# Differential attention with softmax weights left unnormed, value products by tokens and a sub-norm per partition; rotary embedding on a bank copied to SBUF

## The chip, the cores and the metric

The kernel runs on one core of a Trainium2 chip. The metric is device time in microseconds (us) for one execution, the median of several. An execution has five engines that run at the same time, each through its own list of instructions in order: TensorE (PE in the profile, with PEld for its weight loads), VectorE (DVE), ScalarE (ACT), GpSimd (POOL) and SyncE (SP, which issues the DMAs). They wait for each other by semaphores only.

## What is computed

Two transformer stacks on 512 tokens of width 1024, in 32-bit floats: a feed-forward block, a mixing block (differential attention with 8 heads, dilated window attention with 12 heads, gates), a second feed-forward block, then two more layers (window attention with pooling, an MLP, latent attention with a recurrence, an MLP). The change touches the mixing block, whose first part is

```python
qa = partial_rope(qa)            # 8 heads x 2 parts x 64, only the first 16 of 64 rotate
ka = partial_rope(ka)
s = einsum('bqhcd,bkhcd->bhcqk', q, k) / 8        # two score matrices per head
p = softmax(s, axis=-1)
a = p[:, :, 0] - lam * p[:, :, 1]
oa = einsum('bhqk,bkhe->bqhe', a, v)              # v is 128 wide per head
oa = rmsnorm(oa, g_subln) * 0.8                   # over the 128 of each head and token
```

## The kernel before

Activations are kept transposed (features on partitions, 512 tokens along the free axis). Products with weights are made in three matmuls with high and low parts: the weights come from DRAM in chunks, ACT copies a chunk to its high part (`split`, L1733, 128x1024), DVE subtracts for the low part (L1953), and PE runs `mm` (L1532, L1534, L1536). Four split chunks are kept; the split of chunk c+3 is listed when the product of chunk c begins and needs chunk c-1 to be used up.

**Who sets the order.** `work_order()` writes one list of steps. Every engine goes through the same list and picks its part of each step, so the order of the list is the order in each engine's queue. In attention the list is woven from two sources. `pipeline()` advances units of attention; `fill(n)` advances a generator that makes projections (`stream_diff` here) so that PE has other work between the parts of a unit.

**Differential attention** is 32 units (8 heads times 4 blocks of 128 queries), from `diff_unit`. One unit has these steps:

- `diff_score`: PE makes the two 128x512 score matrices in two banks (L1613, each f32 matmul is two passes). DVE takes the maximum of each row (L2104, twice) and scales it (L2106). ACT exponentiates both banks with the row sums accumulated (L1793, twice).
- `diff_soft`: DVE takes the reciprocals of the two sums (L2111), multiplies one with lambda (L2114), scales the first matrix (L2115, 128x512) and adds the second times its factor (L2117, 128x512).
- `turn`: PE transposes the four 128x128 blocks (L1648) into bank 6; ACT copies them to a buffer `et` in `tmps` (L1817).
- `diff_out`: PE multiplies (L1655, four matmuls of two passes) with the value block as stationary and `et` as moving operand, so that the result has the 128 value features on partitions. The four blocks of a head fill one bank.
- After a head, `subln`: ACT copies the bank (L1823) and squares it (L1744), PE sums over partitions with a column of ones (L1589, 8 instructions), DVE makes the inverse root from small 128x4 operands (`rstd`, L1973 to L1984, 12 instructions in a chain), PE spreads it over partitions (L1598, 8 instructions), DVE multiplies (L2179), ACT makes the high part (L1827), DVE the low part (L2182).

`pipeline(..., 1, 1, av=4)` lists, per turn n: score of unit n, one filler step, soft of unit n-1, out of unit n-4, pieces of a finished head's sub-norm, transposes of unit n-2, one filler step. Each turn so takes 2 filler steps.

**The filler** is 22 projections of 128 features (`qk_tile`): for each 24 matmuls into one of two banks, then `rope`. One projection is three steps: 12 matmuls, 12 matmuls, and the rotation. In `rope` DVE multiplies the bank with the cosine table (L2092) and shuffles the bank's partitions (`stream_shuffle`, L2093); then the bank is free. POOL multiplies by the sine table (L2379) and adds (L2385). The two buffers `ftmps` are single: the next rotation starts when the last has ended. Nine filler steps (three projections) are run before unit 0. The same `qk_tile` feeds the dilated attention that follows (`stream_dil`, six projections among four gates), whose own units are not touched.

## Time and profile before

| what | value |
| --- | --- |
| median of 3 runs | 2631.23 us (2629.97 to 2632.77) |
| the profiled execution | 2631.93 us, its span 2630.1 us |
| mean granted TensorE clock | 0.966 |
| PE busy | 2469.7 us, 94% |
| DVE busy | 1321.2 us, 50% |
| ACT busy | 931.6 us, 35% |
| POOL busy | 243.7 us, 9% |
| differential attention, first score to the next stage's first matmul | 461.24 to 701.66 us |

The span runs from the first to the last instruction, and about 1.8 us of the execution lie around it. A row of the trace names an engine, a line of the kernel, the tile written and those read. "Idle before" is time in which the engine stood still ahead of such instructions, with the instruction whose end released it. PE instructions overlap, so the distance from one start to the next is their cost; an f32 matmul shows as two instructions. L numbers are lines of the kernel before.

### The profile page before, as it was taken

To read this page: it belongs to the slowest core of one execution; us is meant where nothing else is said; L and a number is where in the kernel's file an instruction comes from. 1 tells how busy PE (TensorE), PEld (TensorE's weight loads), DVE (VectorE), ACT (ScalarE), POOL (GpSimd) and SP (SyncE) were. 2 spreads that over 40 slices of the span, in tenths; PEclk is the share of its full clock that TensorE was granted. 3 is DMA by queue.
4 is the path that set the end of the run, shared out by engine and by line. 5 is a ranking of instruction groups with operands and counts; after the bars stand their busy time and mean duration, and the time that the engine had idled before them with its cause. 6 is when DMAs were issued, how large, how long until landed. Compare 5 with 4: busy or idle time off the path is not lost.

```text
span 2630.1 us, 28659 instructions
## 1 busy us (share of the span) xinstructions
PE 2469.7 (94%) x11256; PEld 1968.9 (75%) x11256; DVE 1321.2 (50%) x2175; ACT 931.6 (35%) x1446; POOL 243.7 (9%) x180
## 2 busy tenths in 40 slices
PE   8999989989899998999998789999998788999998
PEld 6888877666677787888887557888886556888886
DVE  5423345777554444532436665524445777542433
ACT  4333223343333323322223344413322655431331
POOL 0100102221001001100102200000000211000000
PEclk9999999999899998999998889999998898999999
DMA  4233223111111132223322112322221011332221
GB/s 142 93 100 105 84 86 100 58 44 41 43 62 52 55 102 80 88 86 115 96 83 89 49 40 84 106 96 96 96 88 34 30 32 51 104 104 96 90 99 69
DMA packets 66902, 208.38 MB, mean 79 GB/s; under 512 B 7440, under 2 KB 16144, under 8 KB 66512
## 3 DMA queue, kind: packets, MB, share of 16 engines
q1 hardware_dynamic: 66768, 206.55, 24.5%
q8 instruction: 90, 1.47, 0.2%
q14 instruction: 44, 0.36, 0.0%
HBM read 204.42 MB, written 2.10 MB: 79 GB/s over the span
## 4 chain that ended last, share of the span: by engine, by line
PE 77%; DVE 11%; issue 7%; ACT 3%; POOL 1%; DMA 0%; SPq 0%; DVEq 0%; POOLq 0%; ACTq 0%
PE bank L1532 23%; PE bank L1536 23%; PE bank L1534 22%; DVE wlo L1953 1%; PE bank L1648 1%; DVE sm L2104 1%; ACT whi L1733 1%; PE bank L1569 1%; PE bank L1598 1%; PE bank L1571 1%; PE bank L1573 1%; PE bank L1589 1%; PE bank L1613 1%; DVE eb L2115 1%; PE bank L1639 1%
## 5 line engine op out<-in xcount | busy, mean ns | idle before, releaser
L1953 DVE TENSOR_TENSOR wlo<-wraw,whi 128x1024 fp32r<-128x1024 f32 (+4 forms) x438 | 481.4, 1101 | 570.1 <-ACT whi L1733 568.2
L1532 PE MATMUL bank<-hhi,whi 128*128 128x512 f32 x1744 | 703.1, 403 | 25.9 <-DVE ftmps L2093 13.8
L1534 PE MATMUL bank<-hlo,whi 128*128 128x512 f32 x1744 | 688.7, 395 | 2.5 <-DVE hlo L1959 2.5
L1536 PE MATMUL bank<-hhi,wlo 128*128 128x512 f32 x1744 | 689.1, 395 | 0.7 <-DVE wlo L1953 0.5
L1733 ACT ACTIVATE whi<-wraw 128x1024 fp32r<-128x1024 f32 (+4 forms) x438 | 409.6, 936 | 492.6 <-PE bank L1536 448.0
L1532 PEld LDWEIGHTS bank<-hhi,whi 128*128 128x128 f32 x1744 | 332.9, 191 | 118.5 <-issue 44.5
L1536 PEld LDWEIGHTS bank<-hhi,wlo 128*128 128x128 f32 x1744 | 332.8, 191 | 75.4 <-DVE wlo L1953 3.0
L1534 PEld LDWEIGHTS bank<-hlo,whi 128*128 128x128 f32 x1744 | 333.6, 191 | 74.2 <-DVE hlo L1959 4.5
L1532 PE MATMUL bank<-mhi,whi 128*128 128x512 f32 x576 | 227.1, 394 | 0.1
L1536 PE MATMUL bank<-mhi,wlo 128*128 128x512 f32 x576 | 225.8, 392 | 0.0
L1534 PE MATMUL bank<-mlo,whi 128*128 128x512 f32 x576 | 223.6, 388 | 0.2 <-DVE mlo L2204 0.2
L1536 PEld LDWEIGHTS bank<-mhi,wlo 128*128 128x128 f32 x576 | 108.1, 188 | 25.3
L1534 PEld LDWEIGHTS bank<-mlo,whi 128*128 128x128 f32 x576 | 108.1, 188 | 24.7 <-DVE mlo L2204 0.5
L1532 PEld LDWEIGHTS bank<-mhi,whi 128*128 128x128 f32 x576 | 108.3, 188 | 22.0 <-ACT mhi L1840 0.5
L2358 POOL TENSOR_TENSOR tmps<-tmps 128x512 f32<-128x512 f32 x44 | 56.6, 1286 | 551.0 <-DVE tmps L2005 482.5
L1765 ACT ACTIVATE tmps<-tmps 128x512 f32<-128x512 f32 x64 | 40.5, 632 | 184.1 <-DVE tmps L2023 184.1
L2379 POOL TENSOR_TENSOR ftmps<-ftmps,rs 128x512 f32<-128x512 f32 (+1 forms) x39 | 57.8, 1481 | 508.8 <-DVE ftmps L2093 508.8
L2018 DVE TENSOR_TENSOR ya<-ya,bank 128x512 f32<-128x512 f32 x64 | 43.8, 685 | 115.0 <-PE bank L1536 115.0
L1648 PE MATMUL bank<-ident,eb 128*128 128x128 f32 x400 | 67.3, 291 | 35.6 <-ACT tmps L1817 17.8
L2026 DVE TENSOR_TENSOR mlo<-tmps,mhi 128x512 fp32r<-128x512 f32 x64 | 44.3, 693 | 87.2 <-ACT mhi L1768 87.2
L1793 ACT ACTIVATE eb<-bank,sm 128x512 f32<-128x512 f32 x64 | 43.5, 684 | 118.0 <-DVE sm L2106 118.0
L1648 PEld LDWEIGHTS bank<-ident,eb 128*128 128x128 f32 x400 | 46.3, 147 | 49.8 <-issue 26.8
(344 smaller groups left out, 3266.4 us busy)
## 6 DMA issues: line engine op xcount, KB each, us to landing
wraw<-in_stream SPq DMA_DIRECT2D x343, 512.0 KB, 3.5
wraw<-in_stream SPq DMA_DIRECT2D x40, 192.0 KB, 2.3
wraw<-in_stream SPq DMA_DIRECT2D x22, 256.0 KB, 2.6
wraw<-in_stream SPq DMA_DIRECT2D x8, 320.0 KB, 2.9
xa<-in_x SPq DMA_DIRECT2D x8, 256.0 KB, 5.7
out<-ya SPq DMA_DIRECT2D x8, 256.0 KB, 2.6
m<-in_mask SPq DMA_DIRECT2D x1, 1024.0 KB, 5.1
wraw<-in_stream SPq DMA_DIRECT2D x8, 128.0 KB, 2.0
```

The lines of the kernel that those rows point to most:

```text
L1532: pe.matmul(out, sh, xh, start=first, stop=False)
L1534: pe.matmul(out, sh, xl, start=False, stop=False)
L1536: p = pe.matmul(out, sl, xh, start=False, stop=end and last)
L1648: p = pe.transpose(banks[tb][:, i * 128:i * 128 + 128], src[:, at0:at0 + 128], ident[:, :])
L1733: act.activation(whi[j][:, 0:L], wraw[i][:, 0:L], F.Copy).then_inc(*hi.up(c))
L1765: act.activation(tmps[:, q, :], tmps[:, q, :], F.Square).then_inc(*relu_sq.up((s, f)))
L1793: act.activation(buf(("eb", es[c])), banks[bs[c]][:, :], F.Exp, bias=SM(r, 2 + c), scale=SC, accum_out=SM(r, 4 + c)).then_inc(*exp.up(("di ...
L1953: dve.tensor_tensor(wlo[j][:, 0:L], wraw[i][:, 0:L], whi[j][:, 0:L].bitcast(f32), SUB).then_inc(*lo.up(c))
L2018: dve.tensor_tensor(ya[:, n, :], ya[:, n, :], banks[b][:, :], ADD).then_inc(*x_dve.up((nxt, n)))
L2026: dve.tensor_tensor(ahl[s][1][:, f % 16, :], tmps[:, q, :], ahl[s][0][:, f % 16, :].bitcast(f32), SUB).then_inc(*v_lo.up((s, f)))
L2358: pool.tensor_tensor(tmps[:, q, :], tmps[:, q, :], tmps[:, u, :], MUL).then_inc(*gated.up((s, f)))
L2379: pool.tensor_tensor(s, s, rs[rows, :], MUL).then_inc(*rope_sin.up(key))
```

## The change

1. **Softmax weights unnormed.** ACT's first row sum is kept for the head in a new small tensor `hc`. DVE no longer scales the first matrix (L2115 goes); it multiplies lambda, the first sum and the reciprocal of the second, and adds the second matrix times that to the first. The result is the wanted one times the first row sum; the root mean square norm takes that factor out again, with its small constant scaled by the square of the sum.
2. **One maximum for both banks.** The eight banks are one tensor, and one `tensor_reduce` with two results takes the place of two.
3. **Value products by tokens.** `diff_out` has the `et` block as stationary and the value block as moving operand, so that the result has queries on partitions.
4. **Sub-norm per partition.** After each `diff_out` ACT copies the 128x128 result to `tmps` and squares it into a scratch with the sum accumulated. Per head DVE makes the inverse root from 128x4 operands (`sub_root`: two instructions and the same 11 that `rstd` has after its first), ACT scales the four blocks (`sub_scale`), PE transposes them into bank 6, ACT makes the high part and DVE the low part from that bank with the gain (`sub_turn`). The sums and the spreading on PE, L1823, L1744 and L2179 go.
5. **Rotation on a copied bank.** ACT copies the projection's bank to `ftmps`, which frees the bank; DVE shuffles from there; POOL does sine product, cosine product and sum, three instructions.
6. **A new order.** `pipeline` isn't used for these units. `diff_exp` is a step of its own. Per turn n the list is: score of n, 1.2 filler steps, exponentials of n, transposes of n-1, 1.2 filler steps, out of n-1, soft of n, then the next piece of a finished head's sub-norm (`sub_root` in the turn with the head's last out, `sub_scale` and `sub_turn` in the turn after). A projection is four steps of 6 matmuls, the last with the rotation. Nine filler steps before unit 0 are now two projections and a quarter.

The diff, cut to its core (the marks, the new small tensors, and `root`, which holds the unchanged instructions of `rstd`, are left out; HC(h, name, i, n) are columns of `hc`):

```diff
@@ -585,12 +585,27 @@
         t.freed(("shuffled", key))
         return (name, key)
 
+    def rope_copied(kind, key, t, after):
+
+        r, s = FT.take(), FT.take()
+        put("rope_copied", kind, key, t.bank, r.i, s.i, (t.end, *r.was, *s.was), after)
+        r.free = s.free = (("roped", key),)
+        t.freed(("rope_in", key))
+        return ("roped", key)
+
     def qk_tile(key):
         while QK.full():
             yield
         q = QK.take()
-        t = yield from feat([key], ("h", 1))
-        q.tok = rope(("qk", q.i), key, t, q.was)
+        t = Tile(G.take(), ("h", 1), 128, 0)
+        c = opened(key)
+        for kk in range(0, 8, 2):
+            put("mm", t, c, kk, kk + 2, kk, True)
+            if kk < 6:
+                yield
+        closed.add(c)
+        t.end = ("used", c)
+        q.tok = rope_copied(("qk", q.i), key, t, q.was)
         done[key] = q
         yield
 
...
@@ -612,10 +627,11 @@
         qs, ks = ensure(("qa", h, 0)), ensure(("ka", h, 0))
         es, r = [EB.take(), EB.take()], SMR.take()
         bs = [SB.take(), SB.take()]
-        put("diff_score", u, qs.i, ks.i, [b.i for b in bs], r.i, [e.i for e in es],
-            (qs.tok, ks.tok), [b.was for b in bs], r.was, [e.was for e in es])
+        put("diff_score", u, qs.i, ks.i, [b.i for b in bs], r.i, (qs.tok, ks.tok), [b.was for b in bs], r.was)
         if i == 3:
             qs.free = ks.free = (("score", ("diff", u, 1)),)
+        yield
+        put("diff_exp", u, [b.i for b in bs], r.i, [e.i for e in es], [e.was for e in es])
         for c in range(2):
             bs[c].free = (("exp", ("diff", u, c)),)
         yield
@@ -624,38 +640,45 @@
         yield
         et = T.take()
         yield from turn("diff", u, es[0], 4, et, (("soft", ("diff", u)),))
-        yield
         if i == 0:
-            heads[h] = MB.take()
-        out = heads[h]
-        put("diff_out", u, et.i, out.i, out.was)
+            heads[h] = MB.take(), T.take()
+        out, o = heads[h]
+        put("diff_out", u, et.i, out.i, out.was, o.i, o.was)
         et.free = (("out", ("diff", u)),)
         if i == 3:
-            late.append(subln(h, out))
-
...
+            late.append(subln(h, o))
+
+    def subln(h, o):
+        put("sub_root", h)
+        yield
+        put("sub_scale", h, o.i)
+        tb = TB.take()
+        put("sub_turn", h, o.i, tb.i, tb.was)
+        tb.free = (("oa_lo", h),)
+        o.free = (("sub_turn", h),)
+        yield
+
+    def after_heads():
+        for l in list(late):
+            if next(l, 0) == 0:
+                late.remove(l)
+
+    last, owed = None, 0.0
+    for unit in [diff_unit(h, i) for h in range(8) for i in range(4)] + [None]:
+        for l, fills in ((unit, 1.2), (unit, 0), (last, 1.2), (last, 0), (unit, 0)):
+            if l:
+                next(l, None)
+            owed += fills
+            fill(int(owed))
+            owed -= int(owed)
+        after_heads()
+        last = unit
     fill(10 ** 6)
+    for l in late:
+        for _ in l:
+            pass
+    late.clear()
     va_free = (("out", ("diff", (7, 3))),)
 
     share_banks(6)
...
@@ -1648,13 +1681,21 @@
                         p = pe.transpose(banks[tb][:, i * 128:i * 128 + 128], src[:, at0:at0 + 128], ident[:, :])
                     p.then_inc(*turn.up((stage, u, c)))
                 elif k == "diff_out":
-                    (h, i), et, ob, was = a
+                    (h, i), et, ob, was, o, owas = a
                     w.wait_ge(*turned["diff", (h, i), 0])
                     waits((("tm_act", ("va", 1, 3)), ("tm_dve", ("va", 1, 2)), *was))
                     for kt in range(4):
-                        p = pe.matmul(banks[ob][:, i * 128:i * 128 + 128], va_v[:, kt, h * 128:h * 128 + 128],
-                                      tmps[:, et, kt * 128:kt * 128 + 128], start=kt == 0, stop=kt == 3)
+                        p = pe.matmul(banks[ob][:, i * 128:i * 128 + 128], tmps[:, et, kt * 128:kt * 128 + 128],
+                                      va_v[:, kt, h * 128:h * 128 + 128], start=kt == 0, stop=kt == 3)
                     p.then_inc(*out_mm.up(("diff", (h, i))))
...
+                elif k == "sub_turn":
+                    h, o, tb, was = a
+                    waits(was)
+                    for i in range(4):
+                        w.wait_ge(*sub_scaled[h, i])
+                        p = pe.transpose(banks[tb][:, i * 128:i * 128 + 128], tmps[:, o, i * 128:i * 128 + 128],
+                                         ident[:, :])
+                    p.then_inc(*sub_turn.up(h))
...
                 elif k == "diff_score":
-                    u, q, kq, bs, r, es, toks, bwas, rwas, ewas = a
+                    pass
+                elif k == "diff_exp":
+                    (h, i), bs, r, es, ewas = a
+                    w.wait_ge(*maxed["diff", (h, i)])
+                    if h > 1:
+                        w.wait_ge(*sub_root[h - 2])
                     for c in range(2):
-                        w.wait_ge(*maxed["diff", u])
                         waits(ewas[c])
                         act.activation(buf(("eb", es[c])), banks[bs[c]][:, :], F.Exp, bias=SM(r, 2 + c), scale=SC,
-                                       accum_out=SM(r, 4 + c)).then_inc(*exp.up(("diff", u, c)))
+                                       accum_out=SM(r, 5) if c else HC(h, "sum", i, 1)).then_inc(
+                                           *exp.up(("diff", (h, i), c)))
+                elif k == "diff_out":
+                    (h, i), et, b, was, o, owas = a
+                    at0 = i * 128
+                    w.wait_ge(*out_mm["diff", (h, i)])
+                    waits(owas)
+                    act.activation(tmps[:, o, at0:at0 + 128], banks[b][:, at0:at0 + 128],
+                                   F.Copy).then_inc(*sub_in.up((h, i)))
+                    act.activation(junk[:, :], banks[b][:, at0:at0 + 128], F.Square,
+                                   accum_out=HC(h, "sq", i, 1)).then_inc(*sub_sq.up((h, i)))
+                elif k == "sub_scale":
+                    h, o = a
+                    w.wait_ge(*sub_root[h])
+                    for i in range(4):
+                        s = tmps[:, o, i * 128:i * 128 + 128]
+                        w.wait_ge(*sub_in[h, i])
+                        act.activation(s, s, F.Copy, scale=HC(h, "root", i, 1)).then_inc(*sub_scaled.up((h, i)))
+                elif k == "sub_turn":
+                    h, o, tb, was = a
+                    w.wait_ge(*sub_turn[h])
+                    w.wait_ge(*dcols_set[0])
+                    act.activation(oahi[:, h, :], banks[tb][:, :], F.Copy, scale=DC(16)).then_inc(*oa_hi.up(h))
...
+                elif k == "sub_root":
+                    h, = a
+                    v, u, r = HC(h, "var"), HC(h, "u"), HC(h, "root")
+                    w.wait_ge(*sub_sq[h, 3])
+                    if h > 1:
+                        w.wait_ge(*sub_scaled[h - 2, 3])
+                    dve.scalar_tensor_tensor(u, HC(h, "sum"), EPS, HC(h, "sum"), MUL, MUL).then_inc(*chain.up())
                     w.wait_ge(*chain.now())
-                    dve.tensor_scalar(r.bitcast(i32), r.bitcast(i32), -1.0, 1597463007.0, MUL, ADD).then_inc(*chain.up())
...
-                        dve.scalar_tensor_tensor(u, u, -0.5, v, MUL, MUL).then_inc(*chain.up())
-                        w.wait_ge(*chain.now())
-                        dve.scalar_tensor_tensor(r, u, 1.5, r, ADD, MUL).then_inc(*(rstd.up(norm) if it == 2
-                                                                                    else chain.up()))
+                    dve.scalar_tensor_tensor(v, HC(h, "sq"), 1.0 / 128, u, MUL, ADD).then_inc(*chain.up())
+                    w.wait_ge(*chain.now())
...
+                elif k == "rope_copied":
+                    kind, key, b, ri, si, was, after = a
+                    w.wait_ge(*rope_in[key])
+                    waits(was)
+                    dve.stream_shuffle(ftmps[:, si, :], ftmps[:, ri, :], rope_of(kind)[2]).then_inc(*shuffled.up(key))
                 elif k == "diff_score":
-                    u, q, kq2, bs, r, es, toks, bwas, rwas, ewas = a
+                    u, q, kq2, bs, r, toks, bwas, rwas = a
                     waits(rwas)
-                    for c in range(2):
-                        w.wait_ge(*score["diff", u, c])
-                        dve.tensor_reduce(SM(r, c), banks[bs[c]][:, :], AX.X, MAX).then_inc(*chain.up())
+                    w.wait_ge(*score["diff", u, 1])
+                    assert bs[1] == bs[0] + 1
+                    dve.tensor_reduce(SM(r, 0, 2), bank[:, bs[0]:bs[0] + 2, :], AX.X, MAX).then_inc(*chain.up())
                     w.wait_ge(*chain.now())
                     dve.tensor_scalar(SM(r, 2, 2), SM(r, 0, 2), -SC, None, MUL).then_inc(*maxed.up(("diff", u)))
                 elif k == "diff_soft":
                     u, r, es = a
                     e0, e1 = buf(("eb", es[0])), buf(("eb", es[1]))
                     w.wait_ge(*exp["diff", u, 1])
-                    dve.reciprocal(SM(r, 6, 2), SM(r, 4, 2)).then_inc(*chain.up())
+                    dve.reciprocal(SM(r, 6), SM(r, 5)).then_inc(*chain.up())
                     w.wait_ge(*chain.now())
                     w.wait_ge(*lam[0])
-                    dve.tensor_scalar(SM(r, 7), SM(r, 7), DC(17), None, MUL).then_inc(*chain.up())
-                    dve.tensor_scalar(e0, e0, SM(r, 6), None, MUL).then_inc(*chain.up())
+                    dve.scalar_tensor_tensor(SM(r, 7), HC(u[0], "sum", u[1], 1), DC(17), SM(r, 6), MUL,
+                                             MUL).then_inc(*chain.up())
                     w.wait_ge(*chain.now())
                     dve.scalar_tensor_tensor(e0, e1, SM(r, 7), e0, MUL, ADD).then_inc(*soft.up(("diff", u)))
...
+                elif k == "sub_turn":
+                    h, o, tb, was = a
                     w.wait_ge(*oa_hi[h])
-                    dve.tensor_tensor(oalo[:, h, :], tmps[:, o, :], oahi[:, h, :].bitcast(f32), SUB).then_inc(*oa_lo.up(h))
+                    dve.scalar_tensor_tensor(oalo[:, h, :], banks[tb][:, :], DC(16), oahi[:, h, :].bitcast(f32), MUL,
+                                             SUB).then_inc(*oa_lo.up(h))
...
+                elif k == "rope_copied":
+                    kind, key, b, ri, si, was, after = a
+                    dst, rows, _, tab = rope_of(kind)
+                    r, s = ftmps[:, ri, :], ftmps[:, si, :]
+                    w.wait_ge(*shuffled[key])
+                    w.wait_ge(*at(tab))
+                    w.wait_ge(*before.now())
+                    pool.tensor_tensor(s, s, rs[:, :], MUL).then_inc(*rope_sin.up(key))
+                    before = rope_sin
+                    w.wait_ge(*before.now())
+                    pool.tensor_tensor(r, r, rc[:, :], MUL).then_inc(*rope_r.up(key))
+                    before = rope_r
+                    w.wait_ge(*rope_r[key])
+                    waits(after)
+                    pool.tensor_tensor(dst, r, s, ADD).then_inc(*roped.up(key))
+                    before = roped
```

## Rows read from the trace of the kernel before

**Rows 1.** The page's busy time by engine.

```profile
PE 2469.7 (94%) x11256; PEld 1968.9 (75%) x11256; DVE 1321.2 (50%) x2175; ACT 931.6 (35%) x1446; POOL 243.7 (9%) x180
```

**Rows 2.** Stretches: busy us of each engine, PE clock, DMA share, GB/s.

```profile
461.00:680.00 219.00, 199.79 (x1022) 145.59 (x1020) 173.21 (x376) 88.08 (x190) 52.08 (x40) 0.98 0.15 47
680.00:702.00 22.00, 14.81 (x77) 14.08 (x78) 10.01 (x38) 5.99 (x12) 0.00 (x0) 0.71 0.00 1
```

**Rows 3.** Waits, 455 to 695 us: total us, times, longest us.

```profile
DVE wlo L1953 <- ACT whi L1733: 25.4, 11, 2.5
...
PE bank L1532 <- DVE ftmps L2093: 13.8, 8, 2.6
```

**Rows 4.** Groups of instructions, 455 to 695 us: busy us, mean ns, idle before.

```profile
L2115 DVE TENSOR_SCALAR eb<-eb,sm 128x512 f32<-128x512 f32 x32 | 26.7, 836 | 0.0
L1953 DVE TENSOR_TENSOR wlo<-wraw,whi 128x1024 fp32r<-128x1024 f32 x20 | 24.4, 1220 | 25.4 <-ACT whi L1733 25.4
...
L2093 DVE STREAM_SHUFFLE ftmps<-bank 128x512 f32<-128x512 f32 x21 | 15.3, 728 | 0.0
...
L1598 PE MATMUL bank<-ident,sm 128*128 128x128 f32 x56 | 8.5, 300 | 2.0 <-DVE ftmps L2093 2.0
...
L1589 PE MATMUL bank<-ones,ssb 128*128 128x1 f32 x56 | 7.4, 253 | 0.0
```

**Rows 5.** PE in order of time: half a projection, out, transposes, the next.

```profile
564.51 0.50 PE L1532 MATMUL bank<-hhi,whi 128*128 128x512 f32 x1
...
567.41 1.05 PE L1655 MATMUL bank<-tmps,ya 128*128 128x128 f32 x8
568.30 0.60 PE L1648 MATMUL bank<-ident,eb 128*128 128x128 f32 x4
568.65 0.48 PE L1532 MATMUL bank<-hhi,whi 128*128 128x512 f32 x1
```

**Rows 6.** All engines in order of time, 571 to 582 us, one score onward.

```profile
571.60 1.13 PE L1613 MATMUL bank<-qk 64*128 64x512 f32 x4
...
572.83 1.29 DVE L2104 TENSOR_REDUCE sm<-bank 128x1 f32<-128x512 f32 x2 [1.02 <-PE bank L1613]
...
574.36 0.69 ACT L1793 ACTIVATE eb<-bank,sm 128x512 f32<-128x512 f32 x1 [3.61 <-DVE sm L2106]
...
575.65 1.29 POOL L2379 TENSOR_TENSOR ftmps<-ftmps,rs 128x512 f32<-128x512 f32 x1 [7.70 <-DVE ftmps L2093]
575.70 0.60 ACT L1817 ACTIVATE tmps<-bank 128x512 f32<-128x512 f32 x1
575.78 1.44 DVE L2115 TENSOR_SCALAR eb<-eb,sm 128x512 f32<-128x512 f32 x1
576.18 1.06 ACT L1733 ACTIVATE whi<-wraw 128x1024 fp32r<-128x1024 f32 x1
577.02 1.35 POOL L2385 TENSOR_TENSOR qk<-ftmps 128x512 f32<-128x512 f32 x1
577.26 1.66 DVE L2117 SCALAR_TENSOR_TENSOR eb<-eb,sm 128x512 f32<-128x512 f32 x1
578.84 0.15 DVE L1973 TENSOR_SCALAR sm<-bank 128x4 f32<-128x4 f32 x1
...
581.01 0.16 DVE L1984 SCALAR_TENSOR_TENSOR sm<-newt,sm 128x4 f32<-128x4 f32 x1
```

**Rows 7.** L2117 over the whole run: ns min/median/max, first and last start.

```profile
L2117 DVE SCALAR_TENSOR_TENSOR eb<-eb,sm x32: 750/752/1669, 473.5 to 684.1; 128x512 f32<-128x512 f32 x32
```

**Rows 8.** POOL's product when it meets L1953, at 452 us.

```profile
451.84 2.16 POOL L2379 TENSOR_TENSOR ftmps<-ftmps,rs 128x512 f32<-128x512 f32 x1 [44.30 <-DVE ftmps L2093]
```

**Rows 9.** The only ACT copies of 128x128 out of a bank.

```profile
L1866 ACT ACTIVATE ve<-bank,rcs x4: 360/368/377, 1458.5 to 1459.3; 128x128 f32<-128x128 f32 x4
```

**Rows 10.** PE at the end of the stage.

```profile
699.93 2.08 PE L1598 MATMUL bank<-ident,sm 128*128 128x128 f32 x8 [2.44 <-DVE sm L1984]
```

**Rows 11.** A wait of the dilated stage, 775 to 905 us.

```profile
PE bank L1624 <- POOL qk L2385: 2.9, 1, 2.9
```

More of the change, by code:

```diff
@@ L1243, in program @@
         newt = sb("newt", [128, 8])
[L1244 removed]
+        bank = ctx.enter_context(nc.psum_tensor("bank", [128, 8, 512], f32))
+        banks = [bank[:, i, :] for i in range(8)]
         ahl = {}
```

75 lines of the change are left out of this document (31 added, 44 removed).

## The prediction, made before the change was run

> **What bounds the kernel now.** I first read the page's busy times: PE is busy 94% of the run, so elsewhere the kernel is a matmul kernel and only work that PE does, or waits for, counts [rows 1]. Then the stretches of the stage that is changed. From the first score at 461 us to 680 us PE is busy 199.8 of 219 us and DVE 173.2 [rows 2]. From 680 to 702 the filler has run out: PE is busy 14.8 of 22 us at a granted clock of 0.71, POOL has nothing, and the stage ends with the last spreading [rows 2, 10]. Third, who waits: PE waited 13.8 us for the shuffle that frees a projection's bank, and DVE waited 25.4 us for ACT's split, which stands behind the exponentials in ACT's queue [rows 3]. So PE is short of the bound of its own work because DVE's queue runs late, and the last 22 us have no cover.
>
> PE's own work in the stage, by starts: 12 projection matmuls take 567.41-564.51 = 2.90 us, so a new filler step (6) takes 1.45; out 0.89; transposes 0.35; two scores about 1.1 [rows 5, 6]. 32 units at 2.34 are 75 us; 79 new filler steps 114.5.
>
> **What is removed.** DVE: L2115, 26.7 us in all; the cosine products, 21 of about the shuffle's 0.73, 15 us; a 512-wide multiply per head, about 0.7 each, 5 [rows 4]. One maximum over two banks takes what two took (1.29), so it saves next to nothing [rows 6]. PE: sums and spreading, 7.4 + 8.5 us for seven heads, against 0.4 per head for the new transposes: 13 us less [rows 4, 5]. Turning the operands of the value product costs nothing: eight 128x128 passes either way. The filler: 79 steps remain after the first nine, and 33 turns at 2.4 take 79.2, so the 22 us tail gets cover. If PE were the bound, all this would be worth 40 us or more.
>
> **What is added or moved.** (1) POOL does three instructions of 1.3 us per projection where it did two, some 4.1 us in a row [rows 6]. (2) ACT gets a 0.6 us bank copy per projection, two 128x128 instructions per unit and four per head. The nearest row has 0.37 each, and (1459.3-1458.5)/3 = 0.27 from start to start [rows 9]. (3) The order is much shallower: transposes and out of unit n-1 stand behind the exponentials of n on ACT, and the maximum of n+1 stands behind soft of n on DVE. Before, soft used exponentials of a turn ago and out was four turns behind.
>
> **A turn, walked along the queues.** Score start to exponentials is 574.36-571.60 = 2.76; two exponentials 1.34; the copy of the transposes 0.60; out 0.89. The next score follows: 5.6 us for a quiet turn, against PE's own 5.8 on average, so no slack is left [rows 5, 6]. Into this loop fall 20 projection ends and 19 splits. A projection's end puts a 0.6 bank copy on ACT and a 0.73 shuffle on DVE ahead of soft; a split puts 1.06 on ACT, then 1.22 on DVE (wlo), ahead of soft too where it comes in the second filler place, as two of three do [rows 4, 6]. Soft is 2.6 from the exponentials' start to where DVE is free (1.5 for both sums, 0.45 small ones, 0.67 of L2117), and the next maximum has to wait for it.
>
> **POOL holds DVE up.** L2115 began at 575.78, while POOL ran 575.65 to 576.94, and took 1.44; L2117 began at 577.26 inside POOL's next one and took 1.66, where its minimum is 0.75 [rows 6, 7]. Both ended about 0.3 and 0.55 us after POOL's. The reverse holds: POOL's product took 2.16 when DVE's wlo was in front [rows 8]. So wlo and L2117 each lose about 0.9 us when they meet a rotation, and rotations now last 4.1 of about 11 us. The Trainium skill ("GPSIMD Engine Reference", Key points) says that GpSimd shares its SBUF interfaces with VectorE and contends with instructions with two SBUF inputs; by that rule the small 128x4 and 128x1 ones with two inputs would be held as well, which no row here shows. Counting them would add up to 1.3 us at some turns and make the sum some 10 us larger; I leave them free.
>
> With that the five turns of the repeating pattern (12 filler steps, three projections) come to: quiet 5.6; end of a projection before the exponentials and a split after them 8.2; an end in the second place 7.8; a split in the first place 6.0; end and split in the second place 8.7. The last as an example, from the score's start: transposed copy done 4.7, bank copy 5.2, shuffle 5.95, split 6.1, POOL's first product to 7.3, wlo to 8.3, POOL's second to 9.5, L2117 to 10.1, where a quiet turn's next maximum begins at 6.8. Sum 36.3 for five, 7.25 each; without any holding 33, 6.6 each. 32 turns: 232 us (211).
>
> **Heads.** `sub_root` waits on DVE for the last square: out + 0.95, two ACT instructions and an accumulator read, 0.8. Then 13 small instructions at the pace of rstd (12 in 581.17-578.84 = 2.3) take 2.5 [rows 6], with the next maximum queued behind: 2.2 us late. `sub_turn` stands on PE straight behind the next out and waits for two 128x128 and four scalings on ACT: out + 0.95 + 0.8 + 1.2, then 0.4, where the next score would be at 0.89: 2.4 us of idle PE, less what DVE was late anyway, plus 0.3 for the low part on DVE: 1.6. 3.8 per head, seven heads: 27 us. On the pieces, the nearest small row gives 0.27 to 0.37 each; at 0.69 each (a full-width one) [rows 6] heads would cost 10 us more, at nothing 10 less.
>
> The Trainium skill ("VectorE: DVE Perf Modes", the section on the TRN2 errata) gives ScalarE reading a bank 172 cycles plus one per element and advises pieces of 512 or more; at its 1.2 GHz that estimates 0.25 us for 128 wide, close to the 0.27 pace [rows 9]. It speaks against cutting one 512-wide copy, square and scaling into twelve pieces; with its figure heads would cost 1 us less.
>
> **Start and end.** The nine steps end 4 us sooner, near 457, but score 0 waits for the second rotation: projection end near 455.7, copy 0.6, shuffle 0.73, POOL 4.1, and 0.9 lost to wlo in each of two rotations: score 0 near 463. PE stands about 6 us. The last turn and its chain (two filler places, out, squares, root, scaling, transposes) take 9 us where 22 went.
>
> **Sum.** 463 + 232 + 27 + 9 = 731 against 702: +29. In the dilated stage a score waited 2.9 us for a rotation [rows 11]; that rotation is now 1.3 + 0.6 - 0.7 longer and the four of the burst before it keep 5.8 us apart instead of 5.5: +2 to +3. Some head delays fall in turns already late: -4. So +28 on the profiled execution's 2631.9, 2660; the median shown is 0.7 lower: 2659. DMAs are the same in number and order, SP's queue is untouched.
>
> **Rivals.**
> *Faster: cover wins.* If holding is small and ACT's and DVE's extras fit beside PE's work, the turn is PE's 5.8: 463 + 186 + 2.4 x 7 + 9 = 675, -27: 2604. With the clock that was 0.71 in the tail back up this is its full size. For it: DVE sheds some 45 us, and its lateness is what held PE. Against: the loop over ACT is 5.6 alone. It decides at the second filler place: if wlo and shuffle come ahead of an idle DVE, not ahead of a late soft. Half of it (turn 6.4) is still -5. Chance 0.27.
> *Nothing: no holding.* Turn 6.6: 463 + 211 + 25 + 9 = 708, with overlap about 0 to +8. Chance 0.13, half of it within 0.2%.
> *Worse: the small ones are held as well.* `sub_root`'s 13 and the lambda product wait for POOL, turns near 7.7 and heads near 5: +50 and more, 2685. Chance 0.07.
> *Forecast:* waits across ACT, DVE and POOL take PE's place, +10 to +50. Chance 0.53.
>
> **How the numbers follow.** A measurement tells 0.2% (5.3 us) from no change. Faster: 0.27. Within: 0.06, half the second rival. Slower: 0.67, the rest. The range leaves out about a fifth: its low end is 2608, nearly all of the faster case's mechanism but its last 4 us, its high end 2686, the third rival's value. The likeliest case alone is 2641 to 2682.
>
> **What would show it.** In the profile after: the stage from first score to first value matmul 265 to 275 us long; PE busy near 75% in it with idle ahead of the out product (L1655's successor) ended by ACT's transposed copy, some 1 us per unit, and ahead of the sub-norm's transposes, some 2 us each for eight; DVE busy below 150 us and idle behind exponentials; L2117's successor with a mean above 1.1 us; wlo with a maximum near 2.1; the first score after 462. It is wrong if PE waits on these under 30 us in total, if turns average 6 us, or if the granted clock of the stage drops and does more than the waits.

## The result and the profile after

| what | before | after |
| --- | --- | --- |
| median | 2630.6 us (2628.3 to 2632.8) | 2683.7 us (2683.4 to 2684.3) |
| the profiled execution, its span | 2631.93, 2630.1 us | 2683.37, 2681.6 us |
| mean granted TensorE clock | 0.966 | 0.959 |
| PE, DVE, ACT, POOL busy | 2469.7, 1321.2, 931.6, 243.7 us | 2482.9, 1314.3, 963.7, 287.4 us |
| first score to the next stage's first matmul | 461.24 to 701.66 us | 462.69 to 750.72 us |

The change makes the kernel slower: after over before is 1.0203, with an interval of 1.0191 to 1.0215, or +53 us. The stage itself grew from 240.4 to 288.0 us, +47.6. Another 1.5 us lie ahead of it. In the dilated stage a score waits 7.2 us for a rotation (L1657 for L2481), where it waited 2.9 [rows 11].

The stretches of after, the stage first and then the work ahead of it (busy time and instructions of each engine, then the granted clock, DMA share, GB/s):

```profile
463.00:751.00 288.00, 229.28 (x1019) 154.22 (x1018) 177.24 (x330) 122.35 (x334) 86.52 (x60) 0.90 0.11 35
440.00:463.00 23.00, 15.39 (x68) 12.18 (x68) 9.67 (x11) 6.58 (x8) 9.37 (x6) 0.95 0.28 91
```

The same view of before, from 461 to 702 us:

```profile
461.00:702.00 241.00, 214.60 (x1099) 159.66 (x1098) 183.22 (x413) 94.07 (x202) 52.08 (x40) 0.95 0.14 42
```

PE stands idle for 288.0 - 229.3 = 59 us, where it was 26: +32. The other +15 is PE's busy time, though PE has less to do. This is the clock: 0.90 where it was 0.95. By these two figures, PE was at the slower of its two levels (1.2 GHz, half of 2.4) for about 58 us of the stage, and for about 24 before; that is an estimate. At the slower level the four score instructions that took 1.13 us at 605.33 take 2.08 at 618.95, in the rows in order of time below. Everything else in this comparison is a question of who makes PE wait.

The waits of after from 455 to 770 us (the engine that stood, then whose instruction ended it: us in total, times, the longest):

```profile
ACT eb L1842 <- DVE sm L2190: 99.2, 26, 7.1
DVE ftmps L2182 <- ACT ftmps L1832: 47.6, 20, 5.8
PEld bank L1688 <- ACT tmps L1888: 45.0, 27, 5.2
PE bank L1688 <- ACT tmps L1888: 33.7, 21, 4.8
...
PE bank L1696 <- ACT tmps L1860: 13.0, 8, 6.6
PE bank L1681 <- DVE eb L2201: 11.8, 11, 2.1
...
PE bank L1646 <- POOL qk L2481: 6.0, 1, 6.0
```

PE's waits are new ones beside [rows 3]. The largest is the out product (L1688) for ACT's copy of the transposed weights (L1888), then the sub-norm's transposes (L1696) for ACT's scaling, then the transposes (L1681) for DVE's sum of the two matrices (L2201), and once the first score for a rotation. PEld, the weight load of the same product, stands at the same places. PE no longer waits for the shuffle; in its place DVE waits 47.6 us for the copy that now precedes the shuffle.

The groups of the same stretch (busy us, mean ns of one | idle before):

```profile
L2188 DVE TENSOR_REDUCE sm<-bank 128x2 f32<-128x1024 f32 x32 | 39.0, 1220 | 22.7 <-PE bank L1646 22.7
...
L2201 DVE SCALAR_TENSOR_TENSOR eb<-eb,sm 128x512 f32<-128x512 f32 x32 | 37.3, 1165 | 1.1
...
L2031 DVE TENSOR_TENSOR wlo<-wraw,whi 128x1024 fp32r<-128x1024 f32 x23 | 32.6, 1415 | 24.3 <-ACT whi L1774 24.3
...
L2198 DVE SCALAR_TENSOR_TENSOR sm<-hc,dcols,sm 128x1 f32<-128x1 f32 x32 | 25.7, 804 | 1.1
...
L1850 ACT ACTIVATE tmps<-bank 128x128 f32<-128x128 f32 x32 | 8.9, 277 | 29.4 <-PE bank L1688 29.4
L1852 ACT ACTIVATE junk<-bank 128x128 f32<-128x128 f32 x32 | 8.7, 272 | 0.0
...
L2060 DVE SCALAR_TENSOR_TENSOR hc<-hc 128x4 f32<-128x4 f32 x8 | 5.6, 701 | 3.3 <-ACT junk L1852 3.2
```

The fourth row is the one to stop at: the product with lambda, one element per partition, takes 804 ns in the mean. ACT's small pieces cost what was said, 0.28 and 0.27. The product in its own view (min/median/max in ns):

```profile
L2198 DVE SCALAR_TENSOR_TENSOR sm<-hc,dcols,sm x32: 219/1054/1305, 467.9 to 736.9; 128x1 f32<-128x1 f32 x32
```

And one turn of after in order of time (start, us, engine, idle before in brackets), with a projection's end, a split, and then a finished head:

```profile
602.26 0.68 ACT L1842 ACTIVATE eb<-bank,sm 128x512 f32<-128x512 f32 x1
...
603.59 0.60 ACT L1888 ACTIVATE tmps<-bank 128x512 f32<-128x512 f32 x1
604.06 1.07 ACT L1774 ACTIVATE whi<-wraw 128x1024 fp32r<-128x1024 f32 x1
...
604.24 1.16 PE L1688 MATMUL bank<-ya,tmps 128*128 128x128 f32 x8 [0.68 <-ACT tmps L1888]
604.57 1.27 POOL L2477 TENSOR_TENSOR ftmps<-ftmps,rc 128x512 f32<-128x512 f32 x1
605.17 1.75 DVE L2031 TENSOR_TENSOR wlo<-wraw,whi 128x1024 fp32r<-128x1024 f32 x1 [2.02 <-ACT whi L1774]
...
605.33 1.13 PE L1646 MATMUL bank<-qk 64*128 64x512 f32 x4
...
605.92 2.15 POOL L2481 TENSOR_TENSOR qk<-ftmps 128x512 f32<-128x512 f32 x1
...
607.03 1.06 DVE L2198 SCALAR_TENSOR_TENSOR sm<-hc,dcols,sm 128x1 f32<-128x1 f32 x1
...
608.13 0.75 DVE L2201 SCALAR_TENSOR_TENSOR eb<-eb,sm 128x512 f32<-128x512 f32 x1
608.80 0.15 DVE L2060 SCALAR_TENSOR_TENSOR hc<-hc 128x4 f32<-128x4 f32 x1
...
611.25 1.22 DVE L2188 TENSOR_REDUCE sm<-bank 128x2 f32<-128x1024 f32 x1
...
612.71 0.69 ACT L1842 ACTIVATE eb<-bank,sm 128x512 f32<-128x512 f32 x1 [6.73 <-DVE sm L2190]
...
614.69 2.07 PE L1688 MATMUL bank<-ya,tmps 128*128 128x128 f32 x8 [2.35 <-ACT tmps L1888]
...
618.95 2.08 PE L1646 MATMUL bank<-qk 64*128 64x512 f32 x4
```

The exponentials were done at 603.6, but DVE began nothing on them until the split's low part was over (606.9). The lambda product then stood from 607.03 to 608.09, where POOL's instruction ended at 608.07. The score of 605.33 was ready near 606.5, and its maximum began at 611.25, behind the sum of the two matrices and the 13 small instructions of a head's root (608.80 to 611.3). ACT stood 6.73 us, and PE waited for the copy behind these exponentials.

### The profile page after: what moved, and what is told of

The parts are those of the page before. It is cut to its first block, busy times and chain, and to the rows that moved or that the text cites. A ratio compares the mean times of both kernels' runs of the same rounds, so it can differ in the third digit from the quotient of the medians.

```text
span 2681.6 us, 28469 instructions
## 1 busy us (share of the span) xinstructions
PE 2482.9 (93%) x11160; PEld 1961.6 (73%) x11160; DVE 1314.3 (49%) x2083; ACT 963.7 (36%) x1586; POOL 287.4 (11%) x208
## 4 chain that ended last, share of the span: by engine, by line
PE 76%; DVE 11%; issue 6%; ACT 5%; POOL 2%; DMA 1%; SPq 0%; DVEq 0%; ACTq 0%; POOLq 0%
PE bank L1565 22%; PE bank L1569 22%; PE bank L1567 22%; DVE wlo L2031 1%; PE bank L1681 1%; ACT whi L1774 1%; ACT eb L1842 1%; PE bank L1646 1%; PE bank L1688 1%; PE bank L1602 1%; PE bank L1604 1%; PE bank L1606 1%; DVE sm L2188 1%; PE bank L1709 1%; DVE sm L2198 1%
## 5 line engine op out<-in xcount | busy, mean ns | idle before, releaser
L2031 DVE TENSOR_TENSOR wlo<-wraw,whi 128x1024 fp32r<-128x1024 f32 (+4 forms) x438 | 489.3, 1119 | 562.0 <-ACT whi L1774 560.1
L1681 PE MATMUL bank<-ident,eb 128*128 128x128 f32 x400 | 68.0, 292 | 40.7 <-ACT tmps L1888 17.4
L1681 PEld LDWEIGHTS bank<-ident,eb 128*128 128x128 f32 x400 | 46.4, 146 | 62.6 <-issue 26.6
L2102 DVE SCALAR_TENSOR_TENSOR tmps<-bank,rb 128x512 f32<-128x512 f32 x64 | 44.1, 690 | 64.3 <-PE bank L1569 62.8
```

What stands on the lines that cost most here:

```text
L1681: p = pe.transpose(banks[tb][:, i * 128:i * 128 + 128], src[:, at0:at0 + 128], ident[:, :])
L2031: dve.tensor_tensor(wlo[j][:, 0:L], wraw[i][:, 0:L], whi[j][:, 0:L].bitcast(f32), SUB).then_inc(*lo.up(c))
L2102: dve.scalar_tensor_tensor(tmps[:, q, :], banks[b][:, :], 0.0, rb[:, :], MAX, MUL).then_inc(*relu.up((s, f)))
```

## The experiments

All of them count their stage from the first score to the first matmul of the next stage (240.4 us before, 288.0 after), and "over before" is the ratio to the kernel before on the same chip. Lengths of stages, busy and idle times are those of one profiled execution of each kernel.

**1. The lambda product with one tensor input.** On after:

```diff
-dve.scalar_tensor_tensor(SM(r, 7), HC(u[0], "sum", u[1], 1), DC(17), SM(r, 6), MUL, MUL)
+dve.tensor_scalar(SM(r, 7), HC(u[0], "sum", u[1], 1), DC(17), SM(r, 6), MUL, MUL)
```

> The changed kernel, with the 128x1 product of lambda (L2198, mean 0.80 us, minimum 0.22) as a tensor_scalar with two pointer scalars, so that it has one tensor input. Theory 1 (POOL holds DVE instructions with two tensor inputs, small ones too): its mean falls to about 0.22, but L2201 behind it now meets the same POOL instruction itself, so its mean rises from 1.17 towards 1.5 and the run gains 3 to 8 us. Theory 2 (the small product is slow for another reason, its wait on the reciprocal or a busy queue): its duration stays near 0.8. Theory 3 (being held is free time): duration falls, run unchanged within 2 us.

Measured 2669.6 us, 1.0160 over before (1.0143 to 1.0176), 0.43% or some 11 us less than after. The row now reads:

```profile
L2198 DVE TENSOR_SCALAR sm<-hc,dcols,sm x32: 271/273/277, 466.9 to 725.3; 128x1 f32<-128x1 f32 x32
```

With the same inputs as scalars it is never held. Its own time falls by 32 x 0.53 = 17 us, DVE's busy time in the stage only by 11 (177.2 to 166.4), since `wlo` is held more instead: its mean is 1536 ns where it was 1415. The sum behind the product (L2201) is held more often and for less each time (median 1279 where it was 752, mean 1158 where it was 1165). The stage falls by 11 us too, to 277.2.

**2. The old rotation, in the new order.** On after:

```diff
-        q.tok = rope_copied(("qk", q.i), key, t, q.was)
+        q.tok = rope(("qk", q.i), key, t, q.was)
```

> The changed kernel, with the rotation of before: DVE's cosine product and shuffle from the bank, two POOL instructions instead of three, no copy on ACT. Quarter steps and everything else stay. Theory 1 (POOL's three in a row hold DVE, and ACT's copy delays the exponentials): the first score comes 1.5 to 3 us sooner, turns shorten by 0.4 us, run 12 to 20 us faster than the change, 2664 to 2672. Theory 2 (the shallow order alone makes the loss; DVE's extra 0.69 us per projection costs as much as is saved): within 5 us of 2684.

Measured 2665.1, 1.0135 (1.0120 to 1.0150): 18 us less than after. The first score comes at 459.34, 3.4 us sooner, and the stage is 277.1 us, 10.9 shorter. The lambda product's mean falls from 804 to 645.

**3. The out product one turn later.** On after:

```diff
-    for unit in [diff_unit(h, i) for h in range(8) for i in range(4)] + [None]:
-        for l, fills in ((unit, 1.2), (unit, 0), (last, 1.2), (last, 0), (unit, 0)):
+    for unit in [diff_unit(h, i) for h in range(8) for i in range(4)] + [None, None]:
+        for l, fills in ((unit, 1.2), (unit, 0), (prev, 0), (last, 1.2), (unit, 0)):
...
-        last = unit
+        last, prev = unit, last
```

> The changed kernel with the value product of unit n-2 listed before the transposes of n-1, so that it no longer waits for the copy that ACT makes behind the exponentials of n. One turn is added at the end. Theory 1 (the loop score, maximum, exponentials, transposed copy, out, next score paces quiet turns at 5.6 us and PE's 79 us of waits for the copy are the loss): the waits of the value product for ACT's copy fall below 10 us, turns shorten by 0.7 to 1 us, run 20 to 30 us faster, 2655 to 2663. Theory 2 (DVE's queue paces: maximum behind soft behind split and shuffle): the wait moves to the transposes, which wait for soft, and the run gains under 8 us.

Measured 2666.3, 1.0144 (1.0127 to 1.0161): 15 us less. PE's wait of 33.7 us for L1888 is gone from the out product, and a part of it is found again at the sub-norm's transposes, 39.0 where it was 13.0:

```profile
PE bank L1696 <- ACT tmps L1860: 39.0, 8, 6.6
...
PE bank L1681 <- DVE eb L2201: 13.3, 10, 2.2
```

So a part of the stall went to the next thing that PE asks of ACT too soon, which is `sub_turn`. Of the 17.2 us that the stage is shorter (270.8), 6.4 are idle time of PE (52.3 us are left); the other 10.8 are its busy time, at a clock of 0.92 where it was 0.90.

**4. Part 1 alone, on before.** L2115 goes and lambda takes the first sum in the instruction that was there:

```diff
-dve.tensor_scalar(SM(r, 7), SM(r, 7), DC(17), None, MUL)
-dve.tensor_scalar(e0, e0, SM(r, 6), None, MUL)
+dve.tensor_scalar(SM(r, 7), SM(r, 7), DC(17), SM(r, 4), MUL, MUL)
```

> The kernel before with part 1 alone: DVE no longer scales the first softmax matrix (L2115, 26.7 us), the factor of the second is multiplied by the first sum in the same small instruction. The sub-norm's small constant is not scaled with the sum, as a part of the computation left out. Theory 1 (DVE's queue was what PE waited for before): 8 to 15 us faster than before, 2616 to 2623. Theory 2 (DVE waited for ACT's split anyway, so time saved there is spent waiting): within 4 us.

Measured 2621.2, 0.9974 (0.9960 to 0.9987): 27 us less of DVE's time give 7 us. DVE's wait for the split (L1953 for L1733, 455 to 770 us) rises from 47.1 to 55.5: a part of what is removed turns into waiting.

**5. The sub-norm's transposes one turn later.** On after:

```diff
         put("sub_scale", h, o.i)
+        yield
         tb = TB.take()
```

> The changed kernel with the head's transposes, high and low part listed one whole turn after ACT's scaling, nothing else. Theory 1 (PE stands about 2 us per head straight behind the scalings): PE's waits of L1696 for L1860 (13 us with the weight loads' 15) fall to the last head's 6, run 8 to 14 us faster than the change, near 2670. Theory 2 (the heads fall in turns that DVE has made late anyway, so the wait only moves to the transposes or the out product): under 4 us.

Measured 2666.7, 1.0135 (1.0119 to 1.0150): 18 us less. The stage:

```profile
461.49:735.36 273.87, 217.50 (x1019) 148.82 (x1019) 176.60 (x330) 121.53 (x334) 86.67 (x60) 0.94 0.12 38
```

PE's waits of L1696 fall from 13.0 to 6.6 us, all of it the last head's, but PE still waits 35.9 us for the transposed copy, and its idle time in the stage only falls from 58.7 to 56.4. What falls is its busy time for the same matmuls, from 229.3 to 217.5 us, at a clock of 0.94 where it was 0.90. So by these two executions nearly all of this gain is the clock's, and not the 1.6 us per head of the sum.

**6. Part 5 alone, on before.** The copied-bank rotation (ACT copy, DVE shuffle, three POOL instructions) takes the place of the old one; the order stays.

> The kernel before with part 5 alone: ACT copies the projection's bank, DVE shuffles from there, POOL makes three instructions. The old order, with out four turns behind, stays. Theory 1 (POOL's third instruction holds DVE's two-input ones whatever the order): L2115 and L2117 get means near 1.0 and 1.2, DVE saves 14.5 us of cosine products and loses as much or more, run 3 to 12 us slower than before. Theory 2 (the rotation harms only in the shallow order, and here the bank is freed sooner): 3 to 10 us faster than before, PE's 13.8 us of waits for the shuffle gone.

Measured 2654.1, 1.0084 (1.0066 to 1.0102): +23 us, more than in either theory. The waits that came with it:

```profile
DVE ftmps L2116 <- ACT ftmps L1800: 34.5, 19, 3.2
...
PE bank L1541 <- ACT ftmps L1800: 18.0, 8, 3.0
```

PE waited 13.8 us for the shuffle that freed a projection's bank [rows 3]. Now it waits 18.0 for the copy, and DVE, whose queue holds the shuffle, waits 34.5 for it as well, with the next maximum behind. A copy that is meant to free the bank sooner stands in ACT's queue behind two exponentials: of the stage's 19 copies every one starts straight behind these or behind the copy of the transposes.

**7. Part 1 with the filler spread.** Experiment 4 and `pipeline(..., 0.8, 0.8, av=4)` in place of 1, 1, so that the filler lasts to the end of the stage.

> The kernel before with part 1 alone and 0.8 filler steps where 1 was, at both places, so that the 57 steps last over all 36 turns. The sub-norm's small constant is left unscaled. Theory 1 (a slow last stretch without filler is worth its cover): the 20 us without filler work shrink to under 10, the clock stays up, and the run is 8 to 15 us faster than with part 1 alone, 15 to 20 us faster than before. Theory 2 (turns are paced by DVE, so fewer filler steps per turn leave PE idle in each turn and nothing is won): within 4 us of part 1 alone, 5 to 8 us faster than before.

Measured 2618.7, 0.9952 (0.9937 to 0.9967): -13 us, 6 more than in experiment 4, by ratios whose intervals overlap. From 680 to 700 us PE is now busy 15.8 of 20 us at a clock of 0.88; in experiment 4 it was 15.6 at 0.78. The stage takes 233.6 us here and 232.2 there. So the filler does reach the tail and the clock there is higher, but that this cover shortens anything is not shown: the stage as a whole, with less filler in each turn ahead of the tail, is no shorter.

**8. The four mends together.** After with the edits of 1, 2, 3 and 5.

> The changed kernel with four of its costs undone at once: lambda product with one tensor input, rotation as before, value product one turn later, the head's transposes one turn after the scalings. Theory 1 (the costs are separate): the gains of the single runs add, 11 + 16 + 15 + about 10, and it comes to 2628 to 2634, level with the kernel before. Theory 2 (they overlap, since each only shifts which queue is late): 2640 to 2652, still 0.5 to 0.9% slower than before. Theory 3 (with the waits gone PE's lighter work and the covered tail show): below 2615.

Measured 2617.5, 0.9946 (0.9931 to 0.9962): faster than before by 14 us. The single gains are 0.43 + 0.68 + 0.59 + 0.68 = 2.38%; together they are 1.0203 - 0.9946 = 2.57%. They add up within the intervals, so they are four losses rather than one seen four times. The stage is 226.7 us:

```profile
459.10:685.80 226.70, 203.55 (x1018) 144.68 (x1019) 165.83 (x350) 108.20 (x314) 55.25 (x40) 0.98 0.15 45
```

As many matmul rows as in after take 203.6 us instead of 229.3, and PE stands 23 us instead of 59: of the 61 us between the two stages, idle time is 36 and the clock 26.

**9. As 6, with the cosine product on DVE.** DVE multiplies the copy with the cosine table (0.69 us), and POOL has two instructions as before.

> The kernel before with the copied bank, but the cosine product on DVE, from the copy, so that POOL has two instructions as before. It splits the 22.6 us that the copied bank cost in the old order. Theory 1 (POOL's third instruction is the cost): it comes back to within 5 us of the kernel before. Theory 2 (the copy on ACT is: it queues behind the exponentials, so shuffle and bank come late, PE's 18 us of waits for it): the loss stays, 15 to 25 us slower than before, with DVE's extra 0.69 us per projection on top.

Measured 2656.7, 1.0102 (1.0087 to 1.0117): the loss of experiment 6 stays whole. Against the kernel before, DVE has the same work and POOL the same two instructions; what is new is the copy on ACT, and that DVE reads the copy instead of the bank. These two together cost 26 us. The second has a price as well: POOL's sine product, beside the cosine product that now has both inputs in SBUF, takes 1.79 us in the mean where it took 1.32. Against experiment 6, POOL's third instruction is exchanged for the cosine product on DVE, and nothing is won by it. The waits for the copy are the same:

```profile
DVE ftmps L2116 <- ACT ftmps L1800: 31.6, 19, 3.1
...
PE bank L1541 <- ACT ftmps L1800: 19.0, 8, 3.0
```

**10. Soft ahead of the second filler place.** On the kernel of experiment 8:

```diff
-        for l, fills in ((unit, 1.2), (unit, 0), (prev, 0), (last, 1.2), (unit, 0)):
+        for l, fills in ((unit, 1.2), (unit, 0), (prev, 0), (last, 0), (unit, 1.2)):
```

> The kernel of the four mends with soft of unit n listed ahead of the second filler place, so that DVE does it before the split's low part and the rotation listed there. Theory 1 (soft behind late filler work still delays the next maximum): 4 to 10 us faster than the four mends. Theory 2 (with the out product one turn later PE no longer feels it; the filler's own low parts now come later behind exponentials that DVE must wait for): within 3 us, or up to 5 slower.

Measured 2604.6, 0.9900 (0.9886 to 0.9914): 26 us faster than before, the fastest version here. The split's low part and the projection's instructions now come behind soft in DVE's queue, not ahead of it. The stage:

```profile
459.60:676.30 216.70, 201.69 (x1019) 143.36 (x1019) 169.95 (x350) 108.67 (x314) 59.32 (x40) 0.98 0.16 47
```

PE's own work is what it was in experiment 8; its idle time falls from 23 to 15 us. The mean of the sum of the two matrices falls from 1021 to 867 ns, so it is held less often (experiment 8's row, then this one's):

```profile
L2202 DVE SCALAR_TENSOR_TENSOR eb<-eb,sm 128x512 f32<-128x512 f32 x32 | 32.7, 1021 | 1.1
```

```profile
L2202 DVE SCALAR_TENSOR_TENSOR eb<-eb,sm 128x512 f32<-128x512 f32 x32 | 27.7, 867 | 1.1
```

**11. A full start.** On the kernel of experiment 8, `fill(12)` and 1.15 in place of 1.2, so that three whole projections lie ahead of unit 0.

> The kernel of the four mends with 12 filler steps before unit 0 (three projections, as in the kernel before) and 1.15 per place where 1.2 was. The 3.7 us of PE's wait for the second rotation are covered by the third projection; the steps over the turns are as many as needed. Theory 1 (that wait is lost time): 3 to 4 us faster than the four mends. Theory 2 (less filler per turn gives it back in the turns): within 1.5 us.

Measured 2612.1, 0.9926 (0.9915 to 0.9938), against 0.9946 for experiment 8. The first score doesn't wait, and the stage is 223.2 instead of 226.7. But the third projection was made ahead of it: the first score comes at 461.6 instead of 459.1, and the stage ends at 684.8 instead of 685.8. The intervals overlap, so a gain is not shown.

**12. Experiment 9's rotation on after.**

> The changed kernel, with the cosine product on DVE from the copied bank, so that POOL has two instructions; the copy on ACT stays. With the rotation as before it gained 0.7%; this splits that gain. Theory 1 (POOL's third instruction holds DVE behind it in the shallow order, though it did not in the old one): L2198 and L2201 get shorter on average, most of the gain is here too, 10 to 16 us faster than the change. Theory 2 (the copy on ACT, ahead of the exponentials and ahead of the shuffle, is the cost here too): within 4 us of the change or slower, since DVE has 0.69 us per projection more.

Measured 2675.5, 1.0169 (1.0147 to 1.0191): some 9 us less than after, by intervals that touch, but none of it in the stage. The stage here, and then experiment 2's:

```profile
461.43:749.26 287.83, 230.85 (x1019) 154.62 (x1019) 181.84 (x350) 122.33 (x334) 61.07 (x40) 0.90 0.12 37
```

```profile
459.34:736.46 277.12, 228.88 (x1019) 154.45 (x1019) 182.83 (x350) 111.58 (x314) 52.86 (x40) 0.90 0.12 37
```

The stage takes 287.8 us, as in after (288.0): with one POOL instruction less and the cosine product more on DVE it comes out even. The lambda product is held less (mean 532 ns where it was 804), and DVE has 21 x 0.69 us more to do. Experiment 2 has the same work on DVE and POOL as this one, from the bank and without the copy, and its stage is 10.7 us shorter. So in the new order too the copied bank, and not the third instruction, goes with the stage's loss, as in 9 against the kernel before.

## Why the prediction was right, and where its sizes were off

The forecast was slower, +28 us, with the waits across ACT, DVE and POOL in PE's place. The sign came out so, and so did the mechanism in its main part: PE stands in front of ACT's copies. The size was +53. That lies outside the 2641 to 2682 of the likeliest case, and inside the stated range by 2 us only because that range was drawn out to the third rival's figure, 2685, which had a chance of 0.07. Much of the third rival's mechanism is what was found: the lambda product is held, and of the eight roots four, with turns of 7.6 (7.7 was its figure) and heads of 4.2 (5). So that 2684 falls inside is in part luck.

In the profiled executions the excess over the sum parts as follows: turns and heads 14 us, the end 5, and the -4 for heads that fall in late turns did not show.

- **The quiet turn** (PE's own 75 + 114.5 us are 5.9 per turn and not 5.8, which changes nothing here) was said to take 5.6 us by the loop of score, maximum, exponentials, copy and out. From one maximum's start to the next the first turns take 5.4, 8.6, 8.1 and 5.7 us. The pattern had 5.6, 8.2, 7.8, 6.0 in this order for its first four. Its fifth, 8.7, took 11.5, with the first head's root in it:

```profile
464.81 1.22 DVE L2188 TENSOR_REDUCE sm<-bank 128x2 f32<-128x1024 f32 x1 [4.68 <-PE bank L1646]
...
470.20 1.23 DVE L2188 TENSOR_REDUCE sm<-bank 128x2 f32<-128x1024 f32 x1 [1.24 <-PE bank L1646]
...
478.76 1.22 DVE L2188 TENSOR_REDUCE sm<-bank 128x2 f32<-128x1024 f32 x1
...
486.89 1.21 DVE L2188 TENSOR_REDUCE sm<-bank 128x2 f32<-128x1024 f32 x1
...
492.62 1.22 DVE L2188 TENSOR_REDUCE sm<-bank 128x2 f32<-128x1024 f32 x1 [1.59 <-PE bank L1646]
```

- **Turns in the mean** were taken at 7.25 and the heads at 3.8 each. The last maximum begins at 730.15: 31 turns in 265.3 us. The 17 turns without a head's `sub_root` or `sub_turn` take 7.6, and the 14 with one take 9.7 each, so a head costs 2 x 2.1 = 4.2. That is 14 us more than 31 x 7.25 + 27 = 252, of which the turns are 11 and the heads 3.
- **The step that failed is "I leave them free"**, of the small instructions with two inputs. The lambda product lost 0.58 in the mean against its minimum (804 - 219), 19 us in all, and experiment 1 gets 11 us back, about half of the excess. The Trainium skill ("GPSIMD Engine Reference", Key points), which says that GpSimd contends with VectorE instructions with two SBUF inputs, was right here for one element per partition as for 512. I had worked out its price (10 us, 1.3 at some turns) and then not used it.
- **The end** was put at one turn and 9 us, 16.3. It took 750.72 - 729.0 = 21.7. The last sub-norm's root met the last rotation, and three of its instructions were held, 1.25, 1.12 and 1.10 where 0.15 to 0.17 is their time:

```profile
743.68 1.26 POOL L2474 TENSOR_TENSOR ftmps<-ftmps,rs 128x512 f32<-128x512 f32 x1 [5.76 <-DVE ftmps L2182]
743.71 1.25 DVE L2060 SCALAR_TENSOR_TENSOR hc<-hc 128x4 f32<-128x4 f32 x1
...
745.02 1.26 POOL L2477 TENSOR_TENSOR ftmps<-ftmps,rc 128x512 f32<-128x512 f32 x1
745.19 1.12 DVE L2005 TENSOR_SCALAR hc<-hc 128x4 int32<-128x4 int32 x1
...
746.36 1.27 POOL L2481 TENSOR_TENSOR qk<-ftmps 128x512 f32<-128x512 f32 x1
746.55 1.10 DVE L2010 TENSOR_TENSOR hc<-hc 128x4 f32<-128x4 f32 x1
```

The root took 743.71 to 749.2, 5.5 us, where 2.5 was counted.

- **The start** was right: score 0 near 463 with PE standing 6 us. The first score's row says 462.69 and 6.02.
- **The clock** was named as a way to be wrong, with no term in the sum. It cost less than the waits (26 us of 61 against the mended kernel). The rows at the slower level stand behind PE's longer stops: the out product takes 2.07 after a stop of 2.35 (614.69), and 1.16 after one of 0.68 (604.24). But the price is not in proportion to the idle time. Experiment 1 took 9.0 us of idle time away and 1.8 of busy time, experiment 5 took 2.3 and 11.8. A forecast of an idle PE should carry the clock as a term of its own; which stops cost it was not worked out.
- **The signs to look for.** PE's waits for the transposed copy were 33.7 us for 32 units, about the 1 us each that was said. Those of the sub-norm's transposes were 13.0 with 6.6 at the last head, so 0.9 for each of the other seven, where 2 was said. L2117's successor has a mean of 1165 ns (above 1.1 was said), and wlo a maximum of 1.78 in the stage and 2.21 at its start (2.1). The stage was to be 265 to 275 us (288), PE busy 75% (80%, more because of the clock) and DVE busy below 150 us. DVE shows 177. An instruction that is held counts as busy, and by each line's minimum some 43 us of the 177 are held time, 23 of 183 before: the lambda product 19, the sum of the two matrices 13, the roots 6, `wlo` 4.
- **The reason for the rotation's harm was only half right.** I put it on POOL's third instruction holding DVE, and costed the copy at 0.6 on ACT. Experiments 6 and 9 show +23 and +26 us in the old order with and without that instruction, and 12 against 2 shows 10.7 us of the stage in the new one: the cost goes with the copied bank, where the copy stands behind ACT's other work and DVE's in-order queue behind the copy. Likewise `wlo` was to lose 0.9 whenever it meets a rotation; in the stage it lost 0.56 at most (1776 - 1217 ns), and 3.5 us over its 19.
- **The faster rival** needed a loop that fits beside PE's work. Experiment 10 has all of the change but the rotation, with the lambda product's other form, and reaches 2604.6 once the order has a turn more between ACT's work and PE's need. That this is the rival's 2604 is in part chance, as it is another kernel. But what the change takes away was worth it; the depth of the order, the rotation and the held product took it back.

Still open: what parts 2, 3 and 4 of the change are worth singly, since no run takes them one by one; what POOL's third instruction would cost with nothing put on DVE in its place; and whether experiments 10 and 11 together gain more, which was not tried.

## What to carry to other kernels

Where one list sets the order of all queues, count for each product how long its operand takes through ACT and DVE, and list it a turn later than that; a stall that is mended shows up at the next consumer that is listed too soon, so mend the depth of all. Put short work that the loop waits for (soft, in experiment 10) ahead of the filler's long splits. And moving an engine's work to GpSimd or to a copy on ScalarE is not free because that engine has time left: ask what is ahead of it in that queue, and which small VectorE instructions run beside it.

## What the runs showed of the hardware that was not expected

- Even a VectorE instruction of one element per partition is held to the end of a GpSimd one that is under way or begins with it: of the 32 lambda products of after, 19 ran beside a GpSimd instruction, took 1.03 to 1.31 us and ended within 0.02 us of its end; the 13 beside none took 0.22. A 128x4 one took 1.25 us beside a minimum of 0.15. The same product with its two other inputs as scalars took 271 to 277 ns in all 32 cases.
- One-input instructions are not all safe. A 128x4 integer one took 1.12 above. In experiment 9 a 128x2 one began with POOL's instruction and ended with it:

```profile
583.54 1.27 POOL L2420 TENSOR_TENSOR qk<-ftmps 128x512 f32<-128x512 f32 x1
583.55 1.29 DVE L2127 TENSOR_SCALAR sm<-sm 128x2 f32<-128x2 f32 x1
```

The Trainium skill ("GPSIMD Engine Reference", Key points) also names VectorE's 2-port mode beside two inputs. That mode could be the reason for these two, but no run here shows in which mode an instruction ran.

- The held time counts as DVE's busy time and as no wait of any row, so it is found by minimum against mean in a line's own view, not in the list of waits.
